# Modulation slabs of a two-block transformer: one PSUM bank collects 4, 8 and 12 slabs before it is copied and turned

## The reference

```python
D_MODEL, DEPTH = 1024, 2
# 'c': (1, 1024)   'c_ctx': (1024,)   'mod_w': (2, 1024, 6 * 1024)   'mod_b': (2, 6 * 1024)
mod = jax.nn.silu(c) @ mod_w[i] + mod_b[i]
modc = jax.nn.silu(c_ctx) @ mod_w[i] + mod_b[i]
sh1, sc1, g1, sh2, sc2, g2 = jnp.split(mod[:, None, :], 6, axis=-1)
def _modulate(h, shift, scale):
    return h * (1 + scale) + shift
```

## Time and profile before

| | us |
|---|---|
| median of 3 runs (2490.23 to 2500.96) | 2490.97 |
| the profiled execution's own time | 2492.84 |
| its span, first to last instruction | 2491.1 |
| PE busy (92%) | 2293.1 |
| DVE busy (45%) | 1115.6 |
| ACT busy (23%) | 561.1 |

### The profile page before, as it was taken

How to read it: one execution, slowest core, us unless ns; L and a number is a source line. 1 busy time by engine, 2 the same in 40 slices (tenths; PEclk the granted TensorE clock), 3 DMA queues, 4 the chain that set the end, 5 groups by cost and what they waited for, 6 DMA issues and landing times.

```text
span 2491.1 us, 31355 instructions
## 1 busy us (share of the span) xinstructions
PE 2293.1 (92%) x12364; PEld 1455.2 (58%) x12364; DVE 1115.6 (45%) x2040; ACT 561.1 (23%) x1075; POOL 12.7 (1%) x20
## 2 busy tenths in 40 slices
PE   7999897999999888888999999988999999899998
PEld 3545433444344336464444444378889988888997
DVE  2368624111111116533222222256687776568876
ACT  3233332111111114322111111123331012333101
POOL 0000000000000010000000000000000000000000
PEclk9999898999999999899999999989999998899999
DMA  9169214997999995124999999942244545224443
GB/s 382 68 253 384 106 68 158 380 379 306 417 390 419 429 424 204 68 102 175 424 426 418 417 425 419 421 175 81 90 169 153 193 172 207 98 91 164 158 181 118
DMA packets 48844, 629.86 MB, mean 253 GB/s; under 512 B 5617, under 2 KB 6513, under 8 KB 11249
## 3 DMA queue, kind: packets, MB, share of 16 engines
q1 hardware_dynamic: 43712, 611.27, 60.9%
q10 hardware_dynamic: 2880, 9.44, 0.9%
q0 software_dynamic: 2160, 7.87, 0.8%
HBM read 614.40 MB, written 14.16 MB: 252 GB/s over the span
## 4 chain that ended last, share of the span: by engine, by line
PE 80%; DMA 7%; DVE 7%; ACT 4%; issue 1%; SPq 0%; DVEq 0%; ACTq 0%
PE ps L1390 9%; PE ps L1442 8%; PE ps L1519 5%; DMA ring<-in_ex_up 5%; PE ps L1057 5%; PE ps L1520 5%; PE ps L1521 5%; PE ps L1421 4%; PE ps L1458 3%; PE ps L1525 3%; PE ps L1526 3%; PE ps L1527 3%; PE ps L1346 3%; PE ps L1284 3%; PE ps L1075 2%; PE ps L1692 1%
## 5 line engine op out<-in xcount | busy, mean ns | idle before, releaser
L1521 PE MATMUL ps<-hn_hi,w_lo 128*128 128x256 f32 x992 | 284.8, 287 | 0.0
L1442 PE MATMUL ps<-ring,E 128*64 128x512 f32 x1152 | 253.1, 595 | 20.4 <-DMA ring<-in_ex_up 19.1
L1390 PE MATMUL ps<-ring,E 128*64 128x512 f32 x1024 | 226.0, 594 | 1.7 <-SPq L569 1.7
L1521 PEld LDWEIGHTS ps<-hn_hi,w_lo 128*128 128x128 f32 x992 | 194.5, 196 | 0.0
L1442 PEld LDWEIGHTS ps<-ring,E 128*64 128x64 f32 x1152 | 86.2, 138 | 183.7 <-issue 182.1
L2158 DVE TENSOR_TENSOR E<-E,ps 128x512 f32<-128x512 f32 x18 | 12.4, 689 | 369.3 <-PE ps L1442 369.3
L1390 PEld LDWEIGHTS ps<-ring,E 128*64 128x64 f32 x1024 | 72.5, 137 | 138.2 <-issue 136.0
L1519 PE MATMUL ps<-hn_hi,w_hi 128*128 128x256 f32 x512 | 147.7, 288 | 2.4 <-DVE hn_lo L2279 2.4
L1520 PE MATMUL ps<-hn_lo,w_hi 128*128 128x256 f32 x512 | 147.2, 287 | 0.0
L1519 PE MATMUL ps<-hn_hi,w_lo 128*128 128x256 f32 x480 | 141.2, 294 | 5.5 <-DVE E L2356 3.7
L2247 DVE TENSOR_TENSOR w_lo<-ring,w_hi 128x4096 fp32r<-128x4096 f32 x32 | 141.6, 4425 | 1.1
(11 more groups left out here) (467 smaller groups left out, 3858.3 us busy)
## 6 DMA issues: line engine op xcount, KB each, us to landing
ring<-in_ex_gate SPq DMA_DIRECT2D x64, 2048.0 KB, 12.8
ring<-in_ex_up SPq DMA_DIRECT2D x64, 2048.0 KB, 15.1
ring<-in_ex_down SPq DMA_DIRECT2D x64, 2048.0 KB, 13.3
ring<-in_w_layer SPq DMA_DIRECT2D x56, 2048.0 KB, 7.8
ring<-in_w_static SPq DMA_DIRECT2D x33, 2048.0 KB, 9.2
y_rows<-E ACTq DMA_DIRECT2D x36, 256.0 KB, 8.7
E<-in_w_layer SPq DMA_DIRECT2D x2, 2048.0 KB, 13.2
cat<-in_w_layer SPq DMA_DIRECT2D x2, 2048.0 KB, 17.6
```

What stands on the lines that cost most here:

```text
L1390: ins = pe.matmul(ps[half(u), 2 + w, :], xg[:, k, half(u)], slab(2 * w + u, (KC, DE))[:, k, :], start=k == 0, stop=k == KC - 1)
L1442: ins = pe.matmul(ps[half(u), 2 + w, :], xg[:, k, half(u)], slab(2 * w + u, (KC, DE))[:, k, :], start=k == 0, stop=k == KC - 1)
L1521: return pe.matmul(out, lo, xhi, start=False, stop=last)
```

## The change

The 24 slabs form three sets: 0 to 3, 4 to 11, 12 to 23. Within a set all sums accumulate in bank 6, and each slab's two rows land on their own two partitions of each group of 32. For that the condition stands at columns 22 and 23 of a strip of 54 zero-padded columns, and slab j of a set that starts at j0 takes the 32 columns from 22 - 2 (j - j0): the condition then sits at columns 2 (j - j0) and 2 (j - j0) + 1 of the weights, zeros elsewhere. The first slab's first four matmuls start the bank. After a set ACT copies the bank once, and four matmuls with 8, 16 or 24 columns of a wider `fold` turn it. Set 0 is turned before the projection, set 1 at step 9 ahead of the sum, set 2 at step 22 ahead of the transposes. DVE's bias adds read the new order of columns. ACT's copies in attention come at steps 8 and 20.

```diff
-        condv = sb("condv", [P, KC, 32])
+        condv = sb("condv", [P, KC, 54])
+        MOD_SETS = ((0, 4), (4, 12), (12, 24))
+        def mod_place(q):
+            j0, j1 = MOD_SETS[q]
+            return ((5, 0), (7, 0), (7, 64))[q] + (2 * (j1 - j0),)
@@ ACT
-            act.activation(condv[:, :, 0:2], ...
+            act.activation(condv[:, :, 22:24], ...
-                    for j in range(MOD0):
-                        act.wait_ge(mod_mm, j + 1)
-                        act.activation(mrow, ps[:, 6, :], ACT.Copy).then_inc(mod_ev, 1)
+                    act.wait_ge(mod_mm, MOD0)
+                    act.activation(mrow, ps[:, 6, :], ACT.Copy).then_inc(mod_ev, 1)
-                    if full and 1 <= s <= 24 - MOD0:
+                    if full and MOD0 + s in (12, 24):
                         act.wait_ge(mod_mm, MOD0 + s)
                         act.activation(mrow, ps[:, 6, :], ACT.Copy).then_inc(mod_ev, 1)
@@ PE
-            def mod_sum(j):
+            def mod_sum(q, j):
                 w = take_slab(mod_at(j), (KC, 512))
-                if j:
-                    pe.wait_ge(mod_ev, j)
+                j0, j1 = MOD_SETS[q]
+                at = 22 - 2 * (j - j0)
+                if j == j0 and q:
+                    pe.wait_ge(mod_ev, q)
                 for k in range(KC):
-                    q = k % 4
-                    ins = pe.matmul(ps[32 * q:32 * q + 32, 6, :], condv[:, k, :], w[:, k, :], start=k < 4, stop=k >= 4)
+                    u = k % 4
+                    ins = pe.matmul(ps[32 * u:32 * u + 32, 6, :], condv[:, k, at:at + 32], w[:, k, :], start=j == j0 and k < 4, stop=j == j1 - 1 and k >= 4)
-            def mod_columns(j):
-                pe.wait_ge(mod_ev, j + 1)
-                bank, at = (5, 8 * j) if j < MOD0 else (7, 8 * (j - MOD0))
+            def mod_columns(q):
+                pe.wait_ge(mod_ev, q + 1)
+                bank, at, n = mod_place(q)
                 for m in range(4):
-                    ins = pe.matmul(ps[:, bank, at + 2 * m:at + 2 * m + 2], mrow[:, m * P:m * P + P], cc("fold")[:, 0:2], start=True, stop=True)
+                    ins = pe.matmul(ps[:, bank, at + n * m:at + n * m + n], mrow[:, m * P:m * P + P], cc("fold")[:, 0:n], start=True, stop=True)
@@ PE, start
                     for j in range(MOD0):
-                        mod_sum(j)
-                        mod_columns(j)
+                        mod_sum(0, j)
+                    mod_columns(0)
@@ PE, attention step s
                     if full and 1 <= s <= 24 - MOD0:
-                        if s > 1:
-                            mod_columns(MOD0 + s - 2)
-                        mod_sum(MOD0 + s - 1)
+                        if s == 9:
+                            mod_columns(1)
+                        mod_sum(1 if s < 9 else 2, MOD0 + s - 1)
+                    if full and s == 22:
+                        mod_columns(2)
@@ PE, after the last unit
-                    mod_columns(23)
@@ DVE
             def modulation_first():
-                dve.wait_ge(mod_fold, MOD0)
-                link(mod_bias(0, 0, 4 * MOD0, 5, 0))
+                dve.wait_ge(mod_fold, 1)
+                link(mod_bias(0))
             def modulation_rest():
-                dve.wait_ge(mod_fold, 24)
-                mod_bias(0, 4 * MOD0, 48, 7, 0)
-                link(mod_bias(1, 0, 48, 7, 2 * (48 - 4 * MOD0)))
+                dve.wait_ge(mod_fold, 3)
+                mod_bias(1)
+                link(mod_bias(2))
@@ constants: "fold" is 32 columns wide instead of 16
-    t["fold"] = p % 32 == np.arange(16)[None, :]
+    t["fold"] = p % 32 == np.arange(32)[None, :]
```

More of the change, by code:

```diff
@@ L70 @@
           ("tri_strict", P), ("negtri", P), ("trineg", P), ("band1", P), ("m01", P), ("iota", P),
-          ("cos", NX), ("sin", NX), ("maskc", QT * NCMP), ("visc", QT * NCMP), ("invf", 1), ("eps", 1), ("fold", 16)]
+          ("cos", NX), ("sin", NX), ("maskc", QT * NCMP), ("visc", QT * NCMP), ("invf", 1), ("eps", 1), ("fold", 32)]
 LPARAMS = [("norm_g", 4 * KC), ("pe", 2 * (CB // 2)), ("w2", 2 * 2 * 64)]
@@ L719, in _ @@
             act.wait_ge(setup_done, 1)
-            act.activation(condv[:, :, 0:2], pc("cond").rearrange("p (k c) -> p k c", c=2), ACT.Silu).then_inc(cond_ready, 1)
+            act.activation(condv[:, :, 22:24], pc("cond").rearrange("p (k c) -> p k c", c=2), ACT.Silu).then_inc(cond_ready, 1)
             def trig():
@@ L846, in experts @@
                 if l == 1:
-                    act.wait_ge(mod_fold, 24 + 1)
+                    act.wait_ge(mod_fold, 3 + 1)
                     act.activation(g2B, ps[:, 6:8, :].rearrange("p a b -> p (a b)"), ACT.Copy).then_inc(mod_ready, 1)
@@ L1612, in layer2 @@
                 for q in range(4):
-                    ins = pe.matmul(ps[:, 7, 16 * q:16 * q + 16], hrow[:, q * P:q * P + P], cc("fold"), start=True, stop=True)
+                    ins = pe.matmul(ps[:, 7, 16 * q:16 * q + 16], hrow[:, q * P:q * P + P], cc("fold")[:, 0:16], start=True, stop=True)
                 ins.then_inc(cmp_mm, 1)
@@ L1875, in _, with mod_bias @@
             dve.tensor_scalar(sin2, ang, 3.1415925, -3.1415925, ALU.min, ALU.max).then_inc(trig_ready, 1)
[L1877 to L1880, removed]
+            def mod_bias(q):
+                (j0, j1), (bank, at, n) = MOD_SETS[q], mod_place(q)
+                l, a, b = j0 // 12, 4 * j0 % 48, 4 * j0 % 48 + 4 * (j1 - j0)
+                bias = pc("mod_b", 48 * l + a, b - a).rearrange("p (j m) -> p j m", m=4).unsqueeze(3).broadcast_to([P, j1 - j0, 4, 2])
+                return dve.tensor_tensor(modv[:, l, a:b, :].rearrange("p (j m) c -> p j m c", m=4),
+                                         ps[:, bank, at:at + 4 * n].rearrange("p (m j c) -> p j m c", m=4, c=2), bias, ALU.add)
             def mod_scale(dst, l, at, gain):
```

## The result

The changed kernel took 2481.11 us (median of 8 runs, 2472.14 to 2493.07), the kernel before 2499.46 us (also 8 runs, the three of the prediction among them; 2489.33 to 2506.87). The ratio is 0.9933, 95% interval 0.991 to 0.9956: 16.7 us faster. Timed again later the ratio was 0.9928 (0.9909 to 0.9947). Of all the runs reported here one was slow (2501.88 us, the kernel with idle matmuls in the stage too) and doesn't count in a ratio. The profiled execution has a span of 2479.8 us, 11.3 less than before.

A forecast was written before the change was run, and what follows sets the result against it. TensorE was taken to bound the kernel, with VectorE next in attention and slab transfers at the front. Terms -13.7 + 0.3 - 0.9 - 1.6 - 0.7 = -16.6 us from 2491 gave 2474.4, stated as 2475; range 2468 to 2484.

The forecast's parts named there:

- Step 1: Attention steps 3 to 20: turning and copy go, VectorE then ends last at 4.74 us a step; -13.7 us.
- Rival A: Attention: hand-overs between engines don't hold 4.74 us, a step takes perhaps 5.15; total -9, 2482 us; chance 0.15.
- Rival B: Attention stage: TensorE's short pauses let its clock fall, making the kernel slower; total +6, 2497 us; chance 0.05.
- Rival D: Attention: VectorE is no bound, so TensorE's full saving of 0.98 us a step counts; total -21, 2470 us; chance 0.04.
- Step 2: The remaining attention turnings: +0.3 us at step 9, 0 at step 22; bounds for the pair 0 to 2 us.
- Step 3: Second attention step, TensorE at half clock: without its turning the scores end earlier, -0.9 us; bounds -2.6 and 0.
- Step 4: End of the attention stage: VectorE no longer waits for the last turning, mean sum follows the values; -1.6 us.
- Step 5: Front: four sums without copies, the last held by its slab's landing at 31.9; -1.3 us, half lost at half clock: -0.7.
- rival C: Front: clock falls, fourth sum takes 3.6 us, projections start 0.7 us later; +0.4 instead of -0.7, total 2476 us; chance 0.10.

The follow-up runs named there:

- the kernel with idle matmuls in the stage too: Changed kernel plus normalising multiplies on ScalarE, idle matmuls at the front and in TensorE's waits at attention steps 1 and 21 to 24: 2469.0 us, ratio 0.9892.
- The pair with four multiply-adds: Changed kernel and kernel before, each with four instead of five convolution multiply-adds per attention step: 18 steps took 82.23 and 98.92 us; totals 2467.09 and 2488.32 us.
- the run with attention alone: Changed kernel with the front slab by slab again, attention still in sets of 8 and 12: 18 steps 85.35 us, total 2483.39 us.
- the front alone: Kernel before with only slabs 0 to 3 batched, attention keeping one copy and turning per slab: 18 steps 98.93 us, total 2502.96 us.
- the run with the turning last: Changed kernel with the third set turned after the last unit instead of at step 22: mean sum 1.7 us behind the last values, total 2483.52 us.

## Why the prediction was right, and where it was not

*Step 1, attention steps (-13.7).* Right, in mechanism and size: with step 9's 0.3 the forecast was -13.4, measured -13.6 in all five executions with these sets in attention and DVE's work unchanged (85.32 to 85.36). The 0.2 are the one short step, 0.35 us, that the mean of 4.74 left out. The pair with four multiply-adds shows the change of hand from PE to DVE. Rival A (hand-overs) is out: one wait of 0.26 us in 18 steps. Rival B (the clock falls in the stage) is out for these steps, granted 1.00. Rival D is out by DVE's 4.7 us.

*Step 2, the turnings (+0.3).* Right: 0.34 us at step 9, nothing at step 22 (PE still waits 0.96 us for DVE behind it).

*Step 3, step 2 of attention (-0.9).* Measured -1.2, but this is luck: the same step took 4.80 us (-2.6) in the run with attention alone and in the second profile of the changed kernel. Of the named bounds, -2.6 was met and 0 wasn't.

*Step 4, the end (-1.6).* Right: -1.7 behind unit 21. Four profiles with this order and DVE's work unchanged have 20.9 us there each; before there is one with 22.6 and, with the front alone, one with 23.9, so the run with the turning last, which gives 1.7 back, is the better proof.

*Step 5, the front (-0.7).* The number was hit at the swap matmul (-0.8) by luck, and the working wasn't. The slab landed at 32.1 as foreseen (31.9), but the clock was not 1.00 behind the stretch before it: the sum took 3.6 us, and the projections started 0.6 us later than before, as rival C had it. The -0.7 came back only because 39.1 to 42.5 lay at half clock behind that start, not 38.97 to 44.7. In the second profile nothing came back, and the old front spreads as widely, so -0.7 as the worth of this term is not shown. The idle matmuls show the cause of the slow sum: without the pause of 3 us ahead of it it ran at 2.4 GHz, and the swap matmul came 2.3 us sooner. With the rule that was weighed there, of the Trainium skill (TensorE: Matmul & The Clock Gate, HAM oscillation — how this bites in real kernels), that bursts between DMA waits start cold, the trace agrees: a burst behind a wait for DMA ran at 0.51 of full clock. I should have given C more than 0.10. It was worth 1 us, so the sum stood.

*The base.* I put -16.6 on the 2491 us of three runs; eight runs, the same three among them, have a median of 2499.5. The difference was right (16.7 by the ratio), and the time came out 6 us above the 2475 for that reason. Why the profile's span fell by 11.3 only: behind the mean sum, where no instruction differs, the kernel before took 2206 us, the changed one 2212 and 2205, and the run with the front alone 2214. That is scatter in the same code, not a new wait. Much of it goes along with the clock: by the traces' record of the granted clock, 166 us behind the mean sum lay at half clock in the kernel before, 188 and 168 in the changed one, 195 with the front alone. But not all of it: the run with attention alone had 173 us and took 2214. What else differs is not shown.

## What to carry to other kernels

Before counting what an instruction on the bounding engine is worth, read the next engine's own step from a place where it does not wait: the gain per step was the difference of the two (0.76 us), not the instruction (0.98). When work is moved off the bounding engine, look at all engines' steps together: moving the multiplies (0.48 or 0.62 us a step) from DVE to ACT took 0.23 us off a step, 3.1 in 18, and then the bound was PE again. In a kernel whose executions scatter by 10 us and more, marks inside the trace tell terms of 0.3 us that the time never shows, but only across a stretch at one clock: the 18 steps repeated to 0.04 us, while the swap matmul behind one and the same front moved by 1.5. Profile the old kernel more than once before crediting such a mark to an edit.

## What the runs showed of the hardware

- Turning matmuls with 2, 8, 16 and 24 columns take the same time: 1.05 to 1.07 us for eight passes, in one timeline each.
- A pause of 3.0 us ahead of a sum left it partly or wholly at half clock in each of the six profiles with the batched front and no idle matmuls (2.4, 2.7, 3.1, 3.5, 3.6, 3.6 us instead of 1.9); with idle matmuls in the pause it took 1.92 or 1.93 us in all four.
- The half-clock stretches behind the same old front began at 36.9, 37.9 and 38.8 us in three profiles, and the mark behind it moved from 144.04 to 145.53.
- Transfers that moved 368 GB/s at 0.98 busy share before moved 423 at 1.00 after, when slabs were asked for faster: a busy share near 1 did not mean that the queue was at its rate.
